# A two-layer attention and feed-forward trunk: v as the stationary operand in the dilated units, and three orders

## The reference

```
h = h + concat[dilated heads | differential heads | gated conv](rms_norm(h) @ w_in) @ w_out
g, u = split(rms_norm(h) @ w_up);  h = h + (silu(dwconv(g)) * u) @ w_down
```

## Time and profile before

| | us |
|---|---|
| median of 3 runs | 2381.22 |
| lowest, highest | 2380.68, 2384.05 |
| the profiled execution, its own time | 2382.89 |
| its span, first to last instruction | 2381.1 |
| TensorE busy, share of the span | 2338.4, 98% |
| VectorE busy | 1633.0, 69% |
| ScalarE busy | 990.3, 42% |
| GpSimd busy | 1291.0, 54% |
| mean granted TensorE clock, of full speed | 0.996 |

### The profile page before, as it was taken

One profiled execution on the slowest core, in us unless ns is written; L12 is line 12 of the kernel. 1 busy time (PEld: TensorE's weight loads), 2 busy tenths in 40 slices (PEclk: granted clock), 3 DMA queues, 4 the chain that ended last, 5 costly groups with the idle time before them and its releaser, 6 DMA issues.

```text
span 2381.1 us, 32322 instructions
## 1 busy us (share of the span) xinstructions
PE 2338.4 (98%) x11340; PEld 1952.4 (82%) x11340; DVE 1633.0 (69%) x2648; ACT 990.3 (42%) x1906; POOL 1291.0 (54%) x893
## 2 busy tenths in 40 slices
PE   7999999999999999999999999999999999999998
PEld 6888888877788888888878888888777888888886
DVE  8744677738767777667795457785496677777775
ACT  4344444525434344344524344444254333433343
POOL 3222323448776667777542223242687777677764
PEclk9999999999999999999999999999999999999999
DMA  8957796421333333333399659852223333333332
GB/s 280 246 140 174 187 223 136 118 62 41 101 95 101 96 96 98 97 94 98 131 282 219 168 145 223 191 105 83 62 67 93 98 96 99 99 94 101 99 100 77
DMA packets 162768, 304.47 MB, mean 128 GB/s; under 512 B 11440, under 2 KB 31024, under 8 KB 162608
## 3 DMA queue, kind: packets, MB, share of 16 engines
q1 hardware_dynamic: 129408, 238.20, 32.3%
q0 software_dynamic: 31616, 62.92, 14.7%
q10 hardware_dynamic: 1584, 1.28, 0.2%
HBM read 292.66 MB, written 135.27 MB: 180 GB/s over the span
## 4 chain that ended last, share of the span: by engine, by line
PE 84%; DVE 8%; POOL 4%; issue 2%; ACT 1%; DMA 1%; DVEq 0%; SPq 0%; POOLq 0%; ACTq 0%
PE ps L1048 11%; PE ps L1049 11%; PE ps L1050 11%; PE ps L1019 7%; PE ps L1021 7%; PE ps L1020 7%; PE ps L1126 5%; PE ps L1128 5%; PE ps L1127 5%; PE ps L1367 5%; PE ps L1354 3%; PE ps L1341 2%; PE ps L1342 2%; POOL w_lo L762 1%; DVE q_next L2082 1%
## 5 line engine op out<-in xcount | busy, mean ns | idle before, releaser
L762 POOL TENSOR_TENSOR w_lo<-more_stage,w_hi 128x512 fp32r<-128x512 f32 x304 | 431.8, 1420 | 193.8 <-ACT w_hi L1825 178.4
L727 POOL CAST w_hi<-stage 128x1024 fp32r<-128x1024 f32 x68 | 71.0, 1044 | 650.1 <-PE ps L1021 575.5
L1019 PE MATMUL ps<-x_hi,w_hi 128*128 128x512 f32 x928 | 373.0, 402 | 2.1 <-POOLq L732 1.0
L1021 PE MATMUL ps<-x_hi,w_lo 128*128 128x512 f32 x928 | 362.9, 391 | 0.0
L1020 PE MATMUL ps<-x_lo,w_hi 128*128 128x512 f32 x928 | 361.6, 390 | 0.0
L1825 ACT ACTIVATE w_hi<-more_stage 128x512 fp32r<-128x512 f32 x294 | 181.8, 626 | 290.2 <-PE ps L1050 205.7
L1989 DVE TENSOR_TENSOR h<-ps,h 128x512 f32<-128x512 f32 x400 | 254.1, 683 | 39.7 <-PE ps L1128 30.1
L1048 PE MATMUL ps<-T_hi,w_hi 128*128 128x512 f32 x688 | 267.9, 389 | 1.5 <-DVE q_next L2457 1.5
L1050 PE MATMUL ps<-T_hi,w_lo 128*128 128x512 f32 x688 | 267.7, 389 | 0.0
L1049 PE MATMUL ps<-T_lo,w_hi 128*128 128x512 f32 x688 | 267.7, 389 | 0.0
L762 POOL TENSOR_TENSOR w_lo<-stage,w_hi 128x512 fp32r<-128x512 f32 x146 | 197.7, 1354 | 128.8 <-ACT w_hi L1825 121.5
(11 more groups left out here) (281 smaller groups left out, 4950.5 us busy)
## 6 DMA issues: line engine op xcount, KB each, us to landing
summed<-stream SPq DMA_DIRECT2D x40, 1024.0 KB, 9.3
more_stage<-stream SPq DMA_DIRECT2D x128, 256.0 KB, 2.7
stage<-stream SPq DMA_DIRECT2D x52, 512.0 KB, 3.9
more_stage<-summed SPq DMA_DIRECT2D x100, 256.0 KB, 2.6
summed_downs<-stream SPq DMA_DIRECT2D x16, 1280.0 KB, 10.6
summed<-stream POOLq DMA_DIRECT2D x20, 1024.0 KB, 15.1
summed<-summed POOLq DMA_DIRECT2D x20, 1024.0 KB, 13.2
more_stage<-summed_downs SPq DMA_DIRECT2D x60, 256.0 KB, 2.6
```

The source lines that it names most:

```text
L762: pool.tensor_tensor(block_of(w_lo, n), raw, block_of(w_hi, n).bitcast(f32), ALU.subtract)\
L1019: pe.matmul(out, w_hi[:, s, w], hi, start=start, stop=False)
L1021: return pe.matmul(out, w_lo[:, s, w], hi, start=False, stop=stop)
```

## The change

Five edits:

1. In the dilated units a group is now at most two blocks of both heads, `(b, blocks)`. TensorE turns both heads' blocks side by side (four transposes at most).
2. VectorE divides the probabilities by their sums in place (two products per step behind the reciprocal, one for each head), and `turn_group` waits for the second (`prob_ready`) in the dilated units too.
3. In `attend_group` v (128 columns, both heads) is the stationary operand and the turned probabilities move, 256 columns for each block. The result lies with the dims on partitions. `keep_head` copies each head's rows straight into `h`, without a scale. The transposes of heads of the dilated units, and ScalarE's copies behind them, are gone.
4. ScalarE's `cross_k` of the first step stands behind `keep_head` of that step.
5. On GpSimd `rest_t2` stands ahead of `rest_t3`, and at the start of the program VectorE sums the first squares ahead of `absorb(1)`, with `angles` behind both.

```
 def groups(i, dilated):
-    return [(j, b, min(4, i + 1 - b)) for b in range(0, i + 1, 4) for j in ((1, 0) if dilated else (0,))]
+    most = 2 if dilated else 4
+    return [(b, min(most, i + 1 - b)) for b in range(0, i + 1, most)]
...
 form_t4(layer, pair)
+rest_t2(layer, pair)
 rest_t3(layer, pair)
-rest_t2(layer, pair)
...
 def turn_group(g, i, dilated, layer, u, n):
-    j, b0, blocks = groups(i, dilated)[n]
-    if dilated:
-        pe.wait_ge(exp_done, 2 * g + 2 - j)
-    else:
-        pe.wait_ge(prob_ready, plain_steps(layer, u, i))
+    b0, blocks = groups(i, dilated)[n]
+    pe.wait_ge(prob_ready, g + 1)
...
+    heads = 2 if dilated else 1
     for b in range(blocks):
...
+        for j in range(heads):
+            at = heads * b + j
+            ended = pe.transpose(ps[:, TURNED, at * P:(at + 1) * P],
+                                 prob[:, g % 2, j, (b0 + b) * P:(b0 + b + 1) * P], eye[:, :])
...
 def attend_group(g, i, dilated, layer, u, n):
...
+    for b in range(blocks):
+        if dilated:
+            ended = pe.matmul(ps[:, HEAD, 0:2 * P], v_cur[:, b0 + b, :], turned_blocks[:, 2 * b * P:2 * (b + 1) * P],
+                              start=b0 + b == 0, stop=b0 + b == i)
...
-                        if u and i == turning_step(u):
+                        if u > A_UNITS and i == turning_step(u):
                             turn_heads(layer, u - 1)
...
 def keep_head(g, i, u):
     act.wait_ge(head_done, g + 1)
-    act.wait_ge(share_ready, g + 1)
     if dilated:
...
+        for j, rows in enumerate((low, high)):
+            act.activation(h[rows, u, i * P:(i + 1) * P], ps[rows, HEAD, j * P:(j + 1) * P], ACT.Copy)\
+               .then_inc(head_out, 1)
...
                         if u == 0 and i == 0:
                             keep_q(attended, halves_of_t[1])
-                            cross_k(attended, halves_of_t[1])
...
                         keep_head(g, i, u)
+                        if u == 0 and i == 0:
+                            cross_k(attended, halves_of_t[1])
...
 dve.reciprocal(share[:, at, :], total[:, at, :]).then_inc(share_ready, 1)
...
+if u < A_UNITS:
+    dve.tensor_scalar(p0, p0, share[:, at, 0:1], None, ALU.mult).then_inc(dve_seq, 1)
+    dve.wait_ge(dve_seq, seen(dve_seq))
+    dve.tensor_scalar(p1, p1, share[:, at, 1:2], None, ALU.mult).then_inc(prob_ready, 1)
+    return
...
+partial(0, 0, 1)
+absorb(1, range(KT), g_of)
 angles()
-absorb(1, range(KT), g_of)
 dve.wait_ge(eye_in, 16)
-partial(0, 0, 1)
 roots(0)
```

More of the change, by code:

```diff
@@ L561, in plain_steps @@
         def plain_steps(layer, u, i):
-            return (layer * B_UNITS + u - A_UNITS) * QB + i + 1
+            return step_of(layer, u, i) + 1
         @block.sync
@@ L1359, in attend_group @@
             def attend_group(g, i, dilated, layer, u, n):
-                j, b0, blocks = groups(i, dilated)[n]
+                b0, blocks = groups(i, dilated)[n]
                 count = group_count(layer, u, i) + n
                 pe.wait_ge(turned_out, count + 1)
-                at = j * HEAD_DIM if dilated else 0
-                dims = slice(HEAD_DIM * j, HEAD_DIM * (j + 1)) if dilated else slice(0, P)
-                wide = dims.stop - dims.start
-                for b in range(b0, b0 + blocks):
-                    ended = pe.matmul(ps[:, HEAD, at:at + wide], turned_groups[count % 2][:, (b - b0) * P:(b - b0 + 1) * P],
-                                      v_cur[:, b, dims], start=n == 0 and b == 0, stop=b == i,
-                                      skip_group_check=dilated)
+                turned_blocks = turned_groups[count % 2]
+                for b in range(blocks):
+                    if dilated:
+                        ended = pe.matmul(ps[:, HEAD, 0:2 * P], v_cur[:, b0 + b, :], turned_blocks[:, 2 * b * P:2 * (b + 1) * P],
+                                          start=b0 + b == 0, stop=b0 + b == i)
+                    else:
+                        ended = pe.matmul(ps[:, HEAD, 0:P], turned_blocks[:, b * P:(b + 1) * P], v_cur[:, b0 + b, :],
+                                          start=b0 + b == 0, stop=b0 + b == i)
                 return ended
@@ L1378, in turn_heads @@
             def turn_heads(layer, u):
[L1379 to L1382 removed]
+                pe.wait_ge(heads_ready, layer * B_UNITS + u - A_UNITS + 1)
                 for b in range(QB):
@@ L1690, in keep_turned @@
             def keep_turned(g, i, dilated, n):
-                size = groups(i, dilated)[n][2] * P
+                size = groups(i, dilated)[n][1] * P * (2 if dilated else 1)
                 act.wait_ge(turned_done, turned[0] + 1)
@@ L1703, in keep_mix @@
             def keep_mix(layer, u):
+                if u < A_UNITS:
+                    act.wait_ge(head_out, 2 * (step_of(layer, u, QB - 1) + 1))
+                    act.sem_inc(mix_kept, 2)
+                    return
                 act.wait_ge(heads_turned, seen(heads_turned))
-                by = 1.0 if u < A_UNITS else gain_of(layer, V_SUBLN_SCALED, 0)
+                by = gain_of(layer, V_SUBLN_SCALED, 0)
                 if u >= PENULTIMATE:
@@ L1749, in keep_head @@
                 act.wait_ge(head_done, g + 1)
-                act.wait_ge(share_ready, g + 1)
                 if dilated:
-                    for j in range(2):
-                        act.activation(heads[:, i, HEAD_DIM * j:HEAD_DIM * (j + 1)],
-                                       ps[:, HEAD, HEAD_DIM * j:HEAD_DIM * (j + 1)], ACT.Copy,
-                                       scale=share[:, g % 2, j:j + 1]).then_inc(head_out, 1)
+                    layer = g // (ATTENDING * QB)
+                    if layer and i == 0:
+                        act.wait_ge(h_saved[u], 16 * layer)
+                    for j, rows in enumerate((low, high)):
+                        act.activation(h[rows, u, i * P:(i + 1) * P], ps[rows, HEAD, j * P:(j + 1) * P], ACT.Copy)\
+                           .then_inc(head_out, 1)
                 else:
+                    act.wait_ge(share_ready, g + 1)
                     act.activation(heads[:, i, :], ps[:, HEAD, 0:P], ACT.Copy, scale=share[:, g % 2, 0:1])\
```

10 lines of the change are left out of this document (2 added, 8 removed).

## The result

The changed kernel takes 2401.03 us (median of 5 runs, 2398.76 to 2404.1), the kernel before 2381.22 (five runs, 2378.03 to 2384.51): ratio 1.0079, 95% interval 1.0068 to 1.0090. It is slower by 19 us, and I had forecast 4. The profiled execution is the fastest of the five, 2398.76 with a span of 2396.9.

What follows compares the result with a forecast made beforehand. TensorE, holding 84% of the chain that ends last, was taken as the bound. Terms +10.0 − 3.8 + 3.8 − 3.5 − 0.6 + 0 − 3.0 + 1.5 = +4.4 gave median 2385.6 us, range 2379.5 to 2391.5.

Steps and rivals of the forecast that it cites:

- T2's rest before T3's: Feed-forward pairs: GpSimd starts its rests 0.77 later, hidden in 18 pairs, paid in each layer's first pair: +1.5 us.
- First turns: First dilated step of both layers: TensorE's turn waits 5.0 us for VectorE's products behind a late reciprocal: +10.0.
- the escape: Faster rival, first dilated step: GpSimd's split begins after VectorE's rotation, waits 2.0 instead of 5.0: −5.3, 2375.9; chance 8%.
- the stretched product: Slower rival, dilated steps: GpSimd's split stretches VectorE's products in a few steps: +6.5 to +11, near 2389.5; chance 8%.
- Clock: TensorE's clock falls behind each layer's new first wait, 1.9 us each: +3.8, ends 0 and +5.6.
- the clock falls in the feed-forward too: Slower rival: first pair's wait becomes 1.94 and lowers the clock, +1.9 in each layer: +8.2, 2389.4; chance 10%.
- The wait that goes: Rest of each layer's first dilated step: TensorE's waits for ScalarE's turned copy and VectorE's q vanish: −1.9 each, −3.8.
- Head transposes, small waits, attends: Dilated units: eight head transposes per unit go, −3.5; small waits for turned copies go, −0.6; attends net 0.
- Products in the other steps: Dilated units from step 1 on: VectorE's products hidden beside a projection half; uncovered, 0.3 to 1.5 per step.
- Start: Program start: squares moved ahead shorten VectorE's chain, −3.9, with half a clock fall, +0.9: −3.0, ends −1.5 and −4.4.
- The sum without T2: Whole kernel: all forecast terms except the +1.5 for the order of T2's and T3's rests: +2.9.
- a product is late at a step where a split runs: Slower rival, dilated steps: GpSimd's split makes two products take 1 to 3 us more: +6.5 to +11; chance 8%.

Runs made afterwards that it cites:

- the dilated units alone: Kernel before with the dilated units changed (groups, v stationary, products) and none of the orders: 2386.17 us, ratio 1.0020.
- that without the products: Changed kernel with T3's rest first again and no division by the sums in the dilated units: 2373.49 us, ratio 0.9967.
- T2's rest alone: Kernel before with T2's rest ahead of T3's as the only edit: 2401.52 us, ratio 1.0082.
- that kernel: Changed kernel with T3's rest ahead of T2's again, all other edits kept: 2384.11 us, ratio 1.0009.
- tap late: Kernel before with T2's rest first, plus three unused reciprocals ahead of VectorE's 1024-column tap: 2387.13 us, ratio 1.0021.
- 64 columns: Kernel before in its old order, GpSimd computing 64 columns of T4 twice in each pair: 2382.57 us, ratio 1.0004.
- 192 columns: Kernel before in its old order, GpSimd computing 192 columns of T4 twice in each pair: 2399.84 us, ratio 1.0073.

## Why the prediction was wrong

The sign was right and so were the mechanisms of most terms; one term was mis-sized, because its mechanism was missing, and it is most of the loss.

- **T2's rest before T3's: +1.5 forecast, +19.6 measured.** This is the failed step. The 0.77 of delay was right (0.74 idle; the first pairs' waits grew by 0.72 and 0.78). "In 18 pairs a split ends 1.07 before TensorE asks: hidden" was wrong twice. I checked the split that follows the rests, not each one behind it in GpSimd's queue; and I took its duration as fixed. The next split had the same slack, 1.08, and stood 0.53 ahead of a two-input VectorE operation. A delay of 0.40 left it ahead; one of 0.68, or the 0.77 here, let VectorE's operation begin first, which added 0.97 to this split.
- **First turns: +10.0 forecast, 5.15 and 3.48 of wait measured (8.6).** Layer 1 was right within 0.15. In layer 0 the rotation escaped, and a product paid in its place. I had put the escape and the stretched product down as separate rivals, and they came together. The forecast took layer 0's collision from one execution, and the six kernels with the old start don't have it; what decides it there isn't shown.
- **Clock: +3.8 forecast, 1.7 behind each turn, +3.4.** Right, in the trace; no experiment held the clock apart from the wait. The reason given for it, idle longer than 3.46, was too simple: an idle of 2.35 has the low clock behind it for 6.83 us in the profile of the dilated units alone (46.24) and none in that without the products (1243.14), and one of 1.82 at a first pair has it for 3.41 in that of T2's rest alone (1796.36). So the rival "the clock falls in the feed-forward too" did come true in two other kernels, though in the changed kernel the clock stayed up behind 1.89 and 1.86.
- **The wait that goes: −3.8.** Matched matmuls give −2.2 in each layer. The size is near, but the reason was wrong in part: with the roundings left in place the wait goes too, and in layer 0 the unchanged kernels lose it as well.
- **Head transposes, small waits, attends: −4.1 forecast,** −2.6 in each layer measured, so 1 us more gained; where isn't shown. The cadence of 1.40 stayed.
- **Products in the other steps: nothing forecast.** Right: in the changed kernel only the two first turns wait for one (8.6 us, 2 times).
- **Start: −3.0 forecast, −2.2 in the trace and −3.5 alone.** Inside its ends. GpSimd's split now meets the angles: one of them took 2.44 (29.51 in the changed kernel) where its like took 0.23, so they ended 3 us later than without it. The second squares all but escaped their collision instead (one add of 1.25, the others at 0.69).
- **The sum without T2** was +2.9 against +2.2 measured (1.0009). Without that term the forecast is 2384.1, and 2384.11 was measured. That it is so close is luck: in that kernel the first turns wait 8.0 against 10.0 forecast, and the low clock behind them (3.41 and 6.83 us) costs 5.1 against 3.8.

The rival "a product is late at a step where a split runs" pointed at the mechanism, but I let it stretch VectorE alone and never GpSimd. The earlier trace rows show both engines in one collision; the rows of a pair would have shown the other side.

## What to carry to other kernels

Before a delay is called hidden, every later instruction of that queue must be checked against its consumer, with what it will then run beside. Where GpSimd runs beside a VectorE operation with two operands in SBUF, or one that scales SBUF to SBUF, write down who begins first and by how much: that margin is a slack like any other, and the price of crossing it here was 0.97 us per meeting. And a repeated stretch multiplies: an edit in a loop of 20 deserves the closest look, not the one with the biggest single wait.

## What the runs showed of the hardware

I had known from the earlier trace rows that a GpSimd split can slow VectorE. New to me is that the order of the begins decides who is slowed, for a split of 512 columns and a tap of 1024:

| kernel | GpSimd begins ahead by | split | tap |
|---|---|---|---|
| before | 0.53 | 1.29 | 1.85 |
| tap late | 0.32 | 1.30 | 2.06 |
| 64 columns | 0.08 | 1.29 | 2.30 |
| 192 columns | −0.19 | 2.26 | 1.31 |
| changed | −0.26 | 2.26 | 1.38 |

The engine that begins second is held for about as long as the first still has to run: with 64 columns the split had 1.21 left and the tap took 1.03 longer than the 1.27 that it takes undisturbed; in the changed kernel the tap had 1.12 left, and the split took 0.97 longer. A product of 128 columns does the same (0.28 becomes 2.39 beside a subtraction of 2.34). This agrees with the Trainium skill ("SBUF — State Buffer", SBUF: two separate sides): the port pair that VectorE and GpSimd share is an exclusive lock, whoever starts first has it for the whole instruction, and the other blocks. By that rule the price in a pair could have been worked out beforehand; I had used only the rule that the two contend.
